# Four instead of three seven-product units in each pair of the first block's gates

## The reference, cut to what matters

```python
def first_block(x, ...):
    xn = rms_norm(x, norm_mix_g[l])
    proj = xn @ w_in[l]                       # 2048 x 12296; the last 8192 columns are the gate logits
    xa, xpool, xsc, qkv, f_logit, gate_logits = jnp.split(proj, split_pts, axis=-1)
    y_a, y_b, y_c, y_d = ...                  # four branches, each 512 wide
    ys = jnp.stack([y_a, y_b, y_c, y_d], axis=2)
    branches = jnp.einsum('bskw,kwd->bskd', ys, w_branch[l])
    gates = jax.nn.sigmoid(gate_logits.reshape(b, s, N_BRANCH, d))
    merged = jnp.sum(gates * branches, axis=2)
    x = x + merged @ w_out[l]
    h = rms_norm(x, norm_mlp_g[l]) @ w_mlp_up[l]
    x = x + jnp.square(jax.nn.relu(h)) @ w_mlp_down[l]
```

## Time and profile before

| what | value |
|---|---|
| median of 3 runs | 2437.48 us (2435.96 to 2438.46) |
| profiled execution, its own time | 2437.17 us |
| its span in the trace | 2435.4 us |
| busy TensorE / VectorE / ScalarE | 2426.8 / 1900.6 / 1264.5 us |
| granted TensorE clock | 1.0 of full speed in every slice |

### The profile page before, as it was taken

How to read it: one execution, slowest core, us unless ns; L and a number is a source line. 1 busy time by engine, 2 the same in 40 slices (tenths; PEclk the granted TensorE clock), 3 DMA queues, 4 the chain that set the end, 5 groups by cost and what they waited for, 6 DMA issues and landing times.

```text
span 2435.4 us, 28949 instructions
## 1 busy us (share of the span) xinstructions
PE 2426.8 (100%) x11614; PEld 2029.4 (83%) x11614; DVE 1900.6 (78%) x1798; ACT 1264.5 (52%) x1309; POOL 66.1 (3%) x67
## 2 busy tenths in 40 slices
PE   9999999999999999999999999999999999999999
PEld 8888888888888888888888888788888888888887
DVE  5775598888656795886875658886899989889897
ACT  5545445545444543544543448875655455545553
POOL 0410000000000000000000000000200000000000
PEclk9999999999999999999999999999999999999999
DMA  8555465666655665665665555545565665556654
GB/s 255 173 184 179 156 200 198 205 193 207 237 181 187 195 203 190 198 199 190 196 201 190 205 185 181 157 138 173 173 199 199 197 201 193 205 195 202 202 196 156
DMA packets 233908, 467.19 MB, mean 192 GB/s; under 512 B 14192, under 2 KB 25984, under 8 KB 233390
## 3 DMA queue, kind: packets, MB, share of 16 engines
q1 hardware_dynamic: 232222, 460.09, 58.0%
q10 hardware_dynamic: 1552, 5.25, 0.6%
HBM read 463.20 MB, written 2.10 MB: 191 GB/s over the span
## 4 chain that ended last, share of the span: by engine, by line
PE 97%; DVE 2%; ACT 0%; issue 0%; POOL 0%; DMA 0%; POOLq 0%; ACTq 0%; DVEq 0%
PE acc L1756 11%; PE acc L1752 11%; PE acc L1753 11%; PE acc L465 10%; PE acc L474 10%; PE acc L467 10%; PE acc L494 5%; PE acc L500 3%; PE tp L494 2%; PE sd L494 2%; PE acc L1808 2%; PE acc L1809 2%; PE acc L1812 2%; PE tp L1808 1%; PE sd L1812 1%; PE sd L1809 1%
## 5 line engine op out<-in xcount | busy, mean ns | idle before, releaser
L450 DVE TENSOR_TENSOR wlo<-raw,whi 128x2048 fp32r<-128x2048 f32 (+1 forms) x361 | 813.1, 2264 | 191.6 <-ACT whi L441 189.8
L441 ACT ACTIVATE whi<-raw 128x2048 fp32r<-128x2048 f32 (+1 forms) x361 | 674.5, 1884 | 253.3 <-PE acc L1756 78.3
L465 PE MATMUL acc<-whi,opA_hi 128*128 128x512 f32 x768 | 305.4, 398 | 0.0
L467 PE MATMUL acc<-whi,opA_lo 128*128 128x512 f32 x768 | 300.0, 391 | 0.0
L1752 PE MATMUL acc<-whi,opA_hi 128*128 128x512 f32 x744 | 289.8, 389 | 0.0
L1753 PE MATMUL acc<-whi,opA_lo 128*128 128x512 f32 x744 | 289.5, 389 | 0.0
L1756 PE MATMUL acc<-wlo,opA_hi 128*128 128x512 f32 x744 | 201.4, 389 | 0.1
L474 PE MATMUL acc<-wlo,opA_hi 128*128 128x512 f32 x768 | 192.6, 392 | 0.2 <-DVE wlo L450 0.2
L1019 ACT ACTIVATE whi<-raw 128x1536 fp32r<-128x1536 f32 x79 | 117.5, 1487 | 122.8 <-PE acc L1756 107.2
L2287 DVE TENSOR_TENSOR t_low<-t_sum,t_hi 128x2048 fp32r<-128x2048 f32 x79 | 180.5, 2284 | 0.0
L1752 PE MATMUL acc<-whi,opB 128*128 128x512 f32 x448 | 175.2, 391 | 0.0
(11 more groups left out here) (431 smaller groups left out, 4075.5 us busy)
## 6 DMA issues: line engine op xcount, KB each, us to landing
raw<-in_w_in SPq DMA_DIRECT2D x66, 1024.0 KB, 5.4
raw<-in_w_mlp_up SPq DMA_DIRECT2D x64, 1024.0 KB, 5.2
raw<-in_w_mlp_down SPq DMA_DIRECT2D x64, 1024.0 KB, 5.0
raw<-in_w_in SPq DMA_DIRECT2D x120, 512.0 KB, 4.5
raw<-in_w_gate SPq DMA_DIRECT2D x88, 512.0 KB, 3.8
raw<-in_w_up SPq DMA_DIRECT2D x88, 512.0 KB, 4.8
raw<-in_w_down SPq DMA_DIRECT2D x88, 512.0 KB, 4.6
raw<-in_w_out SPq DMA_DIRECT2D x32, 1024.0 KB, 5.0
```

Of the source, the lines that this page charges most:

```text
L441: eng.activation(whi[:, u % SPL, k, 0:cols], raw[:, u % RAW, k, 0:cols], ACT.Copy).then_inc(hi_split, share(k))
L450: eng.tensor_tensor(wlo[:, u % RAW, k, 0:cols], raw[:, u % RAW, k, 0:cols], whi[:, u % SPL, k, 0:cols].bitcast(F32), ALU.subtract).then_in ...
L465: eng.matmul(acc[:, pair, m, 0:cols], hi[:, kt + i, m * P:(m + 1) * P], whi[:, s, i, 0:cols], start=first and i == 0, stop=False)
L467: eng.matmul(acc[:, pair, m, 0:cols], lo[:, kt + i, m * P:(m + 1) * P], whi[:, s, i, 0:cols], start=False, stop=False)
```

## The change

`BRANCH_SEVEN` gets unit 2 in addition to 3, 5 and 6, so that four of the eight units in each of the six pairs use seven products. A fourth place is added for operand sums: `ad_hi3` lies where the third place of the gates' sums of the second block lies, `ad_lo3` likewise. The making of the four operand sums is spread over other steps: sums at steps 46, 47, 48 and 49, low parts at 47, 48, 49 and 50, in the order of units 5, 2, 3, 6. The wait for the end of the attention's last product (`pv_done`) is now ahead of the sums of step 46, where it was after step 47.

```diff
-BRANCH_SEVEN, LATER = (3, 5, 6), 3
+BRANCH_SEVEN, LATER = (2, 3, 5, 6), 3
...
-                [at(f"ad_hi{k}", kb, [P, 4, P], F32R) for k, kb in enumerate((c1, c1 + 2, c1 + 32))]]
+                [at(f"ad_hi{k}", kb, [P, 4, P], F32R) for k, kb in enumerate((c1, c1 + 2, c1 + 32, c0 + 4.25))]]
...
-                [at(f"ad_lo{k}", kb, [P, 4, P], F32R) for k, kb in enumerate((c1 + 4, c1 + 6, c1 + 34))]]
+                [at(f"ad_lo{k}", kb, [P, 4, P], F32R) for k, kb in enumerate((c1 + 4, c1 + 6, c1 + 34, c1 + 40))]]
...
-        BRANCH_ORDER = (2, 0, 1)
+        BRANCH_ORDER = (2, 0, 1, 3)
+        BRANCH_STEPS, BRANCH_LOWS = (46, 47, 48, 49), (47, 48, 49, 50)
         FIRST_STEPS = ((2, 2), (3, 1), (3, 2))
+        FIRST_LOWS = ((2, 3), (3, 2), (3, 3))
...
-                    if g == G_GATE0 + NB and j in (0, 1, 3):
-                        n = (0, 1, 3).index(j)
+                    if g * UN + j in BRANCH_LOWS:
+                        n = BRANCH_LOWS.index(g * UN + j)
                         sums_high(1, BRANCH_ORDER[n], n)
...
+            def branch_sums(s):
+
+                if s in BRANCH_LOWS:
+                    n = BRANCH_LOWS.index(s)
+                    operand_low(1, BRANCH_ORDER[n], n)
+                if s in BRANCH_STEPS:
+                    n = BRANCH_STEPS.index(s)
+                    if n == 0:
+                        dve.wait_ge(pv_done, 3)
+                    operand_sums(1, BRANCH_SEVEN[BRANCH_ORDER[n]], n, 0)
+
...
                     side(g * UN + j)
-            def branch_sums(n):
-                operand_sums(1, BRANCH_SEVEN[BRANCH_ORDER[n]], n, 0)
-
-            dve.wait_ge(pv_done, 3)
-            branch_sums(0)
+                    branch_sums(g * UN + j)
             dve_g = G_GATE0 + NB
             for j in range(NB):
                 lo_unit(dve, dve_g, j)
                 side(dve_g * UN + j)
                 if j:
                     branch_part(0, j - 1, R_GATE0 + NB + j - 1, dve_g * UN + j)
-                if j in (0, 1, 3):
-                    n = (0, 1, 3).index(j)
-                    operand_low(1, BRANCH_ORDER[n], n)
-                if j in (0, 2):
-                    branch_sums(1 + j // 2)
+                branch_sums(dve_g * UN + j)
```

More of the change, by code:

```diff
@@ L628, in sums_made @@
             return SUMS1 + (x + 1 if p.op == 0 else PLACES + 2 * p.chunk[0] + x + 1)
-        BRANCH_ORDER = (2, 0, 1)
+        BRANCH_ORDER = (2, 0, 1, 3)
+        BRANCH_STEPS, BRANCH_LOWS = (46, 47, 48, 49), (47, 48, 49, 50)
         FIRST_STEPS = ((2, 2), (3, 1), (3, 2))
+        FIRST_LOWS = ((2, 3), (3, 2), (3, 3))
         def first_low_after(c, j):
-            return [x for x, (d, k) in enumerate(FIRST_STEPS) if (d, k + 1) == (c, j)]
+            return [x for x, step in enumerate(FIRST_LOWS) if step == (c, j)]
         OUT2 = ([(K_WIN0, n, True, True) for n in range(UN)]
```

## The result

The changed kernel takes 2447.58 us (median of five runs, 2445.33 to 2448.16). The kernel before took 2436.81 us beside it (five runs, 2435.96 to 2438.46). The ratio is 1.0042, with a 95% interval of 1.0028 to 1.0057: slower by over 0.2%, as forecast, but 3.2 us later than the 2444.4 us predicted and 0.6 us above the range. The forecast started from a median of 2437.5 us for the kernel before; against the 2436.8 us measured beside the change, the difference is 10.8 us where 6.9 was predicted, so the true miss is 3.9 us and the higher start hid 0.7 of it. The profiled execution took 2447.58 us with a span of 2445.7 us (before 2437.17 and 2435.4), so its span is the one to take apart: 10.3 us more.

A forecast was written before the change was run, and what follows sets the result against it. TensorE was taken to bound the kernel; turns longer by 2.48 + 2.22 + 2.22 = 6.9 us took the profiled 2437.17 us to 2444.1, and 0.3 us to the median gave 2444.4 us, range 2440.5 to 2447.

The forecast's parts named there:

- What goes: TensorE, one unit changed in each of six pairs: 0.68 us less each, 4.08 us in all if nothing else moves.
- What is added, and the walk: VectorE gets 4.38 us more per pair; TensorE waits 1.0 and 2.6 us; turns 2.48, 2.22 and 2.22 us longer.
- rival 3: VectorE's sets of sums lengthen back to back, or waits inside pairs add up: 1 us more a turn, 2447.4 us; chance 0.06.
- Rival 1: In the pairs, TensorE and VectorE drift apart by less than the work in hand: 2433.4 us, not slower; chance 0.06.
- Rival 2: First pair's lateness is caught before the second, unit 1's high part ready sooner: 2441.6 us; chance 0.13.
- The operand sums: Before the first pair, VectorE's added set and moved steps fit its 7.68 us of idle time: -0.14 us, bounds 0 and +0.5.
- Rival 4, the clock: TensorE's clock falls to its lower level after the six new waits: 6 x 5.44 = 32.6 us, 2477 us; chance 0.02.

The follow-up runs named there:

- e8_matmuls_only: Kernel before, with three of the 24 matmuls of unit 2 left out in each of the six pairs and nothing added: 2432.75 us, 0.9985.
- e10_early: Changed kernel, at pair ends two sums before the next low part, combine's last step and two sums behind; ScalarE's next high part between sigmoids: 2433.43 us, 0.9988.
- e2_three: Changed kernel's new steps for the operand sums (46 to 48, low parts 47 to 49), with three sevens in each pair as before: 2435.86 us, 0.9996.
- e1_fill: Changed kernel, with five matmuls whose result nothing reads put on TensorE ahead of the first branch unit of each turn: 2443.72 us, 1.0028.
- e9b_longer: Changed kernel, with the last instruction of combine done three times instead of once after each turn's second pair: 2458.54 us, 1.0090.
- e4_second: Changed kernel, with four sevens only in the second pair of each turn: 2443.49 us, 1.0032.

## Why the prediction was right in its walk and wrong in its time

**What goes** (4.08 us): right. 18 matmuls fewer, and e8_matmuls_only gave 1.36 us a turn.

**What is added, and the walk**: right to 0.05 us in each turn. In the times of the second turn, VectorE of the kernel after:

```profile
435.74 2.28 DVE L450 TENSOR_TENSOR wlo<-raw,whi 128x2048 fp32r<-128x2048 f32 x1
437.94 1.22 DVE L2272 TENSOR_TENSOR t_sum<-raw 128x1024 f32<-128x1024 f32 x1
444.52 1.22 DVE L2272 TENSOR_TENSOR t_sum<-raw 128x1024 f32<-128x1024 f32 x1
...
466.47 4.48 DVE L450 TENSOR_TENSOR wlo<-raw,whi 128x2048 fp32r<-128x2048 f32 x2
470.88 0.68 DVE L2343 TENSOR_TENSOR vw<-tp,q_sum 128x512 f32<-128x512 f32 x1
473.45 0.69 DVE L2400 TENSOR_TENSOR acc<-acc,q_sum 128x512 f32<-128x512 f32 x1
478.57 2.29 DVE L450 TENSOR_TENSOR wlo<-raw,whi 128x2048 fp32r<-128x2048 f32 x1 [2.62 <-ACT whi L441]
...
516.28 0.69 DVE L2400 TENSOR_TENSOR acc<-acc,q_sum 128x512 f32<-128x512 f32 x1
```

A seven-product unit takes 444.52 - 437.94 = 6.58 us also when two follow each other, which takes rival 3 away. From unit 1 to `combine` it is 35.14 us (walked 35.12), to the first sum 2.57 (2.59), from unit 1 to the second pair's first sum 80.54 (80.55). The two rests of the earlier trace rows ahead of the sums are gone: neither 466.47 nor 470.88 has a bracket. TensorE waited 0.98 us for the second pair in that turn (walked 1.0), and came to the first branch unit 518.35 - 475.01 - 40.80 = 2.54 us later than matmuls alone would take it (walked 515.87 - 513.2 = 2.67, where the text says 2.6):

```profile
475.01 0.47 PE L1754 MATMUL acc<-whi,opA_hi 128*128 128x512 f32 x1 [0.98 <-ACT gates L1249]
```

These 2.54 us are not all idle: 0.54 of them were lost inside the pair, whose last matmul starts at 516.12 and not at 475.01 + 40.80 - 0.23 = 515.58, and from that matmul's recorded end to 518.35 the engine is idle for 1.84 us.

**Rival 1**, all hidden: fell. It describes e10_early instead, once the order at the pair's end is changed. That both say 2433.4 us is chance: the rival is 4.1 us below 2437.5, e10_early 3.3 us below the 2436.7 measured beside it.

**Rival 2**, caught up: fell. The rest behind the fourth sum is 2.62 us, as it was before (2.63); the chain of sigmoid and high part moved along with it.

**The operand sums**: right in effect (e2_three), and nearly in the way. VectorE still rested 3.60 us there, of the 7.68 of the earlier trace rows, where the prediction left 2.5 (from 303 to 305.48).

**Rival 4, the clock: this is the step that failed.** The text had the mechanism and set it aside, with a chance of 0.02 and nothing of it in the sum; the traced execution lost 3.27 us to it, and e1_fill, which keeps the clock up, is 3.9 us faster. Two things were wrong. It was argued away with "It waited up to 1.1 us elsewhere" at a clock of 1.00; that bears on the new waits of 1.0 us, where indeed nothing fell, but not on those of 2.6 us, which left TensorE idle for 1.84 to 1.88 us. And it was priced as all or nothing, six waits at 5.44 us each, 32.6 us, which made it look impossible. Measured in the profiled execution, two of six waits had it, at 1.63 us each. A case of one to three falls at some two microseconds would have put the time at an estimated 2446 to 2450 us (2444.4 and 2 to 6 us) and the range a little higher. The Trainium skill (TensorE: Matmul & The Clock Gate, "What's actually happening") says that an idle TensorE goes back to half rate; the trace agrees (0.50 of the full clock in the steps of 1 us above), and the sentence deserved more than 0.02 where the walk itself yielded waits more than twice as long as any seen.

Shown by runs: that the 3.3 us are the clock's (e1_fill), and that with a wait of 4.4 us the clock fell every time and for longer (e9b_longer: three of three turns in the trace, and the same mean clock in all four runs). The number of falls differs from run to run of the kernel after, by the granted clocks given under e1_fill. Open: why the same wait led to a fall in one turn and not in another. What each fall cost in the runs without a trace is not shown.

## What to carry to other kernels

When work moves from the engine that bounds to another, compare the two engines' periods from hand-over to hand-over, with every rest bound to a third engine counted as busy: VectorE at 85% of the turn could not take 8% more, because its period between two pair ends was 42.8 us against TensorE's 40.8. First ask what order at the hand-over lets the waiting engine go soonest and leaves no rest behind; the same change was worth +10.8 us (1.0042, 1.0028 to 1.0057) or -3.3 us (0.9988, 0.9979 to 0.9997) by that alone, the falls of the clock that came with the first included. And a new wait of about two microseconds in TensorE's stream is priced with a possible fall of its clock, as a case of its own with a size from rows, not only with its own length.

## What the runs showed of the hardware that was not expected

- After a wait of 1.84 to 1.88 us the clock's fall came when TensorE was already back at work: the granted clock read 1.00 up to the restart and 0.50 from 0.4 and 0.8 us later (kernel after, second and third turn) or 1.4 us later (e4_second). In a wait of 4.4 us it fell in the wait itself (e9b_longer, 0.52 in the step from 524 us, with the restart at 525.15), and was low from the first matmul.
- Its price was small and steady in the three falls traced: 1.63 to 1.65 us each after 1.84 to 1.88 us of idle time (some nine matmuls, up to 0.43 us apart), 2.4 to 2.8 us after 4.4 us. It ended under dense work by itself.
- Five small multiplications, 1.4 us of work that left 0.55 us of the wait idle, kept the clock up in all three turns, and at a mean of 1.000 in all seven runs (e1_fill).
- Coming back from a wait cost a little even at full clock: at 411.18 of the kernel after, the first distance between starts is 0.34 us and the second 0.24 instead of 0.227.
